# The second half of a retention gate, moved from the attention stage into a Strassen stage of its own

## The chip, the cores and the metric

The program runs on one core of one Trainium2 chip. The metric is the device time of one execution in microseconds (us). An execution has a TensorE queue (PE in the profile; its weight loads are PEld), VectorE (DVE), ScalarE (ACT), GpSimd (POOL), and SyncE (SP), which here only issues transfers. Every wait between engines is a semaphore written by hand in the source.

## The reference

A layer of a language model on 1024 tokens of width 1024, in fp32: a norm, one wide projection `proj = hn @ w_in`, a retention branch and a sliding-window attention branch, each with gates, and an MLP behind them.

```
hn = rms_norm(h, mix_norm_g)
proj = hn @ w_in
rq, rk, rv, rg, sq, sk, sv, gr, gs = split(proj)   # widths 512, 512, 1024, 1024, 1024, 256, 256, 1024, 1024
y_ret = rms_norm(retention(rq, rk, rv)) * silu(rg)
y_swa = sliding_window_attention(sq, sk, sv, sinks)   # 16 query heads, 4 key heads, window 128, 16 meta tokens
merged = sigmoid(gr) * (y_ret @ w_ret_branch) + sigmoid(gs) * (y_swa @ w_swa_branch)
h = h + merged @ w_out
h = h + square(relu(rms_norm(h) @ w_up)) @ w_down
```

The change concerns `rg`, of which `silu(rg)` is stored in a DRAM tensor `gates`.

## The kernel before

**Arithmetic.** An fp32 product is made of three matmuls (`three`, L1144 to 1151): high part by high part, high by low, low by high. So each weight tile exists twice, as WH (rounded by a ScalarE copy) and WL (the rest, a VectorE subtraction); both are rings of eight tiles of 128 x 512. A slab is 512 columns of `w_in`, k is one of eight blocks of 128 input channels, and a slab by all tokens is 64 steps of three matmuls of 512 columns: 192.

**Stages.** The first slab (RQ) runs to about 51 us. From there to 290.8 us comes the Strassen stage: three pairs of slabs (`NSG = 3`: RK with the keys and values of the attention, the two halves of RV, the two halves of SQ), each as the seven products of one Strassen step (`st_product`, L1216) of four bands f, four k and three matmuls, 48 matmuls a product. Quarters of the weights are loaded by SP into PX, PY, PZ and RAW; VectorE forms their sums in PX, PZ and PT (`add_y`, `st_sum`, `add_raw`) and WL (`st_lo`), ScalarE forms WH (`st_hi`). Results are copied out of the banks by ScalarE (`evict`), or summed by VectorE (`result`) in the tiles SA and SB, and stored by GpSimd (`store_st`) to `proj`. Next comes the retention stage, to about 430 us, which weaves the two GR slabs (SLAB_B) between its blocks n = 0 to 7; then `BR = 36` gate steps ahead; then the attention stage from about 457 to 720 us. The last stages, to 1608 us, are the two branches, `w_out`, and the MLP as Strassen products of larger size.

**The attention stage.** It has 68 steps T. A step of TensorE is: its share of the gate slabs GS, GS + 512, RG, RG + 512 (`SLAB_D = 3` to 6; `gate_steps`, L119, spreads 4 x 64 - 36 = 220 gate steps of three matmuls evenly, three or four in each T), the values of a group of two pairs (`values`, odd T), transposes of the next queries or keys, the transposes of the probabilities of pair T - 3 (`transpose_p(T - LAG)`, L1431 and L1434), and the scores of pair T (`scores(T)`, L1417). A pair is two of 16 heads in one of eight blocks of 128 tokens, 64 pairs. VectorE does the minimum over sinks and scores (L2716), the reciprocal of the sum (L2749), the low part of the transposed probabilities (L2724), the splits of the gate weights (L2252), and for `rg` the product of the gate (`tanh` + 1) x value. ScalarE does exponentials (L2012), tanh and casts.

GpSimd's loop, in this order in each T (L1017 to 1043): scale the two heads' probabilities by the reciprocal (L1023); store finished gate tiles (L960); in T = 9, 17, ..., 49 load a table of distances; in T = 20, 28, 36, 44 load KV (L969); in odd T from 7 two transfers that add values to RT from YA (L1042). SP copies the scaled probabilities PR to PW (`copy_p`, L783), which `transpose_p` waits for. These transfers are issued in program order, and an issuing engine does nothing else meanwhile.

## Time and profile before

| | us |
|---|---|
| time, median of 3 runs | 1610.26 (1610.2 to 1610.85) |
| the profiled execution | 1610.03 |
| its span, first to last instruction | 1608.2 |
| mean granted clock | 1.00 |
| TensorE busy | 1599.7 (99%) |
| VectorE busy | 1045.2 (65%) |
| ScalarE busy | 773.2 (48%) |
| GpSimd busy | 420.9 (26%) |

The span lies inside the time; what is around it is start and end of the program. Busy times are those of the profiled execution. A matmul is shown longer than the distance to the next, since matmuls overlap in the array; their distance is read from the starts in the timeline. A transfer's busy time on its engine is the time of issuing it; its landing is told apart.

### The profile page before, as it was taken

What the parts mean: (1) busy time and instruction counts of PE and PEld (TensorE: products, weight loads), DVE (VectorE), ACT (ScalarE), POOL (GpSimd) and SP (SyncE); (2) the same over time, 40 slices, a digit from 0 to 9 for tenths busy, and PEclk for the clock granted to TensorE, in tenths of its full rate; (3) what the DMA queues carried; (4) which work ended last, traced back from release to release, by engine and by line L of the source; (5) the groups of instructions that cost most, each with busy time, mean ns of one, the idle gap of its engine ahead of it and who ended that gap; (6) DMA issues with size and microseconds to landing.
All of it is one profiled execution on the core that took longest, in us unless ns stands there. A gap on an engine that the chain in (4) does not pass through costs nothing.

```text
span 1608.2 us, 22700 instructions
## 1 busy us (share of the span) xinstructions
PE 1599.7 (99%) x7966; PEld 1338.7 (83%) x7966; DVE 1045.2 (65%) x2015; ACT 773.2 (48%) x1587; POOL 420.9 (26%) x604
## 2 busy tenths in 40 slices
PE   9999999999999999999999999999999999999999
PEld 7888888888888888888888888888888888888887
DVE  7984656655657787766555338866666556756675
ACT  7633243545456777672122136655555444444442
POOL 0111011211348898864211000121121222100000
PEclk9999999999999999999999999999999999999999
DMA  8433332654435666568553223444444399733452
GB/s 300 180 101 120 100 117 72 234 181 167 156 117 152 171 177 165 159 153 269 174 186 96 66 82 115 136 166 150 144 150 158 118 322 351 243 94 97 154 180 92
DMA packets 129825, 255.95 MB, mean 159 GB/s; under 512 B 15040, under 2 KB 50288, under 8 KB 129712
## 3 DMA queue, kind: packets, MB, share of 16 engines
q1 hardware_dynamic: 84416, 130.64, 25.9%
q0 software_dynamic: 45008, 123.72, 23.2%
q8 instruction: 64, 1.05, 0.3%
q14 instruction: 49, 0.40, 0.1%
q10 hardware_dynamic: 288, 0.14, 0.0%
HBM read 159.67 MB, written 69.47 MB: 142 GB/s over the span
## 4 chain that ended last, share of the span: by engine, by line
PE 96%; DVE 2%; ACT 1%; DMA 1%; POOL 1%; issue 0%; DVEq 0%; ACTq 0%
PE bank L1146 29%; PE bank L1151 29%; PE bank L1150 29%; PE bank L1417 2%; PE bank L1449 1%; PE bank L1431 1%; PE bank L1189 0%; PE bank L1549 0%; PE bank L1335 0%; PE bank L1466 0%; PE bank L1499 0%; DVE WL L2252 0%; PE bank L1453 0%; POOL PR L1023 0%; PE bank L1434 0%
## 5 line engine op out<-in xcount | busy, mean ns | idle before, releaser
L1146 PE MATMUL bank<-WH,ADH 128*128 128x512 f32 x448 | 174.3, 389 | 0.0
L1150 PE MATMUL bank<-WH,ADL 128*128 128x512 f32 x448 | 174.3, 389 | 0.0
L1151 PE MATMUL bank<-WL,ADH 128*128 128x512 f32 x448 | 174.3, 389 | 0.0
L1146 PE MATMUL bank<-HN,WH 128*128 128x512 f32 x384 | 153.0, 398 | 0.1
L2178 ACT CAST ADH<-ARAW 128x512 fp32r<-128x512 f32 x112 | 69.6, 621 | 169.7 <-PE bank L1151 152.5
L1023 POOL TENSOR_SCALAR PR<-PR,RC 128x272 f32<-128x272 f32 (+1 forms) x128 | 138.4, 1216 | 47.5 <-DVE RC L2749 47.3
L1151 PE MATMUL bank<-HN,WH 128*128 128x512 f32 x384 | 150.2, 391 | 0.0
L1150 PE MATMUL bank<-HN,WL 128*128 128x512 f32 x384 | 150.1, 391 | 0.0
L3003 DVE TENSOR_TENSOR ADL<-ARAW,ADH 128x512 fp32r<-128x512 f32 x112 | 77.5, 692 | 97.2 <-ACT ADH L2178 97.2
L1146 PE MATMUL bank<-SOPH,WH 128*128 128x512 f32 x256 | 99.8, 390 | 0.0
L1151 PE MATMUL bank<-SOPL,WH 128*128 128x512 f32 x256 | 99.6, 389 | 0.0
L1150 PE MATMUL bank<-SOPH,WL 128*128 128x512 f32 x256 | 99.6, 389 | 0.0
L1146 PEld LDWEIGHTS bank<-WH,ADH 128*128 128x128 f32 x448 | 84.1, 188 | 17.6
L1151 PEld LDWEIGHTS bank<-WL,ADH 128*128 128x128 f32 x448 | 84.1, 188 | 17.5
L1150 PEld LDWEIGHTS bank<-WH,ADL 128*128 128x128 f32 x448 | 84.1, 188 | 17.3
L2012 ACT ACTIVATE PR<-PR,NM 128x273 f32<-128x273 f32 (+1 forms) x128 | 64.3, 504 | 55.2 <-DVE NM L2716 54.9
L1151 PEld LDWEIGHTS bank<-HN,WH 128*128 128x128 f32 x384 | 72.1, 188 | 16.0
L1146 PEld LDWEIGHTS bank<-HN,WH 128*128 128x128 f32 x384 | 72.3, 188 | 13.1 <-DVE TB L2744 0.5
L1150 PEld LDWEIGHTS bank<-HN,WL 128*128 128x128 f32 x384 | 72.3, 188 | 11.9
L2144 ACT CAST WH<-XS 128x512 fp32r<-128x512 f32 x64 | 39.1, 616 | 87.4 <-DVE XS L2970 45.1
L1104 POOL DMA_DIRECT2D uop<-UA x48 | 26.0, 541 | 192.8 <-ACT UA L2231 96.0
L1146 PE MATMUL bank<-A,WH 128*128 128x512 f32 x192 | 74.9, 390 | 0.0
(360 smaller groups left out, 4308.1 us busy)
## 6 DMA issues: line engine op xcount, KB each, us to landing
ARAW<-uop SPq DMA_DIRECT2D x112, 256.0 KB, 3.1
uop<-US POOLq DMA_DIRECT2D x64, 256.0 KB, 2.9
WRAW<-in_w_up SPq DMA_DIRECT2D x15, 1024.0 KB, 6.2
PW<-PR SPq DMA_DIRECT2D x56, 272.0 KB, 3.0
RAW<-in_w_in SPq DMA_DIRECT2D x58, 256.0 KB, 4.1
gates<-TB POOLq DMA_DIRECT2D x48, 256.0 KB, 2.7
uop<-UA POOLq DMA_DIRECT2D x48, 256.0 KB, 3.1
proj<-SA POOLq DMA_DIRECT2D x36, 256.0 KB, 2.6
```

Source lines behind the costliest of these rows:

```text
L1023: pr = pool.tensor_scalar(keys, keys, RC[:, b, hl:hl + 1], None, ALU.mult)
L1104: pool.dma_start(uop[t, f], src[:, :]).then_inc(ust_a, 16)
L1146: mm = pe.matmul(bank, ahi, bhi, start=first, stop=False, skip_group_check=onto)
L1150: pe.matmul(bank, alo, bhi, start=False, stop=False, skip_group_check=onto)
L1151: return pe.matmul(bank, ahi, blo, start=False, stop=last, skip_group_check=onto)
L1417: mm = pe.matmul(B[2 + hl][:, 0:NKEY if n else NKEY0], QT[:, 2 * p + hl, :], KTS[:, part, g, keys_of(n, hl)], start=part == 0, stop=part == 1)
L1431: pe.transpose(B[4][:, c * P:(c + 1) * P].bitcast(F32R), PW[:, b, key:key + P], IDR[:, :])
L1449: pe.matmul(B[7][:, :], v, tile[:, sl, :, :].rearrange("p h t -> p (h t)"), start=opens, stop=True, skip_group_check=not opens)
L2012: e = act.activation(part, part, ACT.Exp, scale=-1.0, bias=NM[:, T % 3, hl:hl + 1], accum_out=RS[:, T % 3, hl:hl + 1])
L2144: act.copy(WH[:, wslot(q), :].rearrange("p (k n) -> p k n", k=4), up_src(f, t)).then_inc(uw_hi, 1)
L2178: act.copy(ADH[:, n % 4, :], ARAW[:, n % 4, :]).then_inc(da_hi, 1)
L3003: dve.tensor_tensor(ADL[:, n % 4, :], ARAW[:, n % 4, :], ADH[:, n % 4, :].bitcast(F32), ALU.subtract)\
```

## The change

`SLAB_E` falls from 7 to 6: the attention stage holds three gate slabs instead of four, `NGT = 24` gate tiles instead of 32, and 3 x 64 - 36 = 156 gate steps instead of 220, two or three in each T instead of three or four. The columns RG + 512 to RG + 1023 are computed behind the three pairs of the Strassen stage and ahead of the retention stage, as a fourth pair `GX` of two halves of 256 columns. Its seven products (`gx_product`) have two bands f of 128 output columns, four k and three matmuls each, 24 matmuls a product. Here the weights are the stationary operand and 512 tokens move through, so that a result is a tile of 128 output columns by 512 tokens, as `gates` holds it. SP loads quarters of 256 columns (PYX, RAW, PXX, PZX); the sums, splits, evictions, tanh and products of this part run on the engines that did the same before, with tiles SA and SB, and GpSimd stores eight tiles to `gates[5]` (`store_gx`), between the loads of the first retention tiles (`load_rt`), one of which moves behind a store. The split of the first retention slab (SLAB_B) moves behind it. In block n = 0 the retention stage has two added waits on TensorE and two on ScalarE. Semaphore targets and the ring's numbering follow.

```
--- before.py
+++ after.py
-SLAB_B, SLAB_D, SLAB_E, SLAB_F, SLAB_H = 1, 3, 7, 11, 13
+SLAB_B, SLAB_D, SLAB_E, SLAB_F, SLAB_H = 1, 3, 6, 10, 12
...
+GX, GXF = NSG, 2
+NSX = NSG + 1
+W0 = NSX * NST
 BR = 36
+
+NGT = 8 * (SLAB_E - SLAB_D)
...
-    n = 4 * KT * 8 - BR
+    n = NGT * KT - BR
     return range(BR + n * T // STEPS, BR + n * (T + 1) // STEPS)
...
-ASIDE = (4, 5, 6)
+ASIDE = (4, 5)
...
+GX_EVICT = {0: 0, 2: 1, 3: 2}
+GX_SUM = {1: 0, 4: 1, 5: 2}
+GX_OUT = {1: 0, 4: 1, 5: 2, 6: 3}
+GX_HALF = {1: 0, 4: 1, 5: 0, 6: 1}
...
+        PXX, PTX = at("PXX", O_M, [4, 256]), at("PTX", O_M + 4096, [2, 256])
+        PYX, PZX = at("PYX", O_M + 8192, [4, 256]), at("PZX", O_M + 16384, [4, 256])
...
+            if g == GX:
+                return (PXX[:, k, :], RAW[:, k, 0:256], PTX[:, k % 2, :], PXX[:, k, :], PTX[:, k % 2, :],
+                        PZX[:, k, :], PTX[:, k % 2, :])[t]
...
+        def st_w(tile, g, t, k):
+
+            return tile[:, st_n(g, t, k) % WS, 0:256 if g == GX else SL]
+
+        def gx_act_of(t, k):
+
+            if t in QUAD:
+                return SHI[:, QUAD[t], k, :], SLO[:, QUAD[t], k, :]
+            k, lo = (k + 4, SL) if t == 6 else (k + 4 * t, 0)
+            return HN[:, 0, k, lo:lo + SL], HN[:, 1, k, lo:lo + SL]
+
+        def gx_bank(t, f):
+
+            return B[4 + f] if t % 2 == 0 else B[2 + f]
+
+        def gx_tile(t, f):
+
+            return SB[f] if t in (2, 5) else SA[2 + f] if t == 6 else SA[f]
...
+            done = 20 * (NSG - 1)
+            c0, c1 = COL_RG + SL, COL_RG + SL + 256
+            sp.wait_ge(ps_x, done + XT4 + 4)
+            sp.dma_start(PYX[:, :, :], quarter(c1, 0, 256)).then_inc(py_full, 16)
+            sp.wait_ge(ps_x, done + ZS + 4)
+            for k in range(4):
+                sp.dma_start(RAW[:, k, 0:256], w_in[SL + k * P:SL + (k + 1) * P, c0:c0 + 256]).then_inc(raw_full[k], 16)
+            sp.wait_ge(ps_x, done + XT6 + 4)
+            sp.dma_start(PXX[:, :, :], quarter(c0, 0, 256)).then_inc(px_full, 16)
+            sp.dma_start(PZX[:, :, :], quarter(c1, 1, 256)).then_inc(pz_full, 16)
+            sp.wait_ge(ps_x, 20 * GX + ZS + 4)
...
-            w_from = [w_cols(w_in, COL_GS), w_cols(w_in, COL_GS + SL), w_cols(w_in, COL_RG), w_cols(w_in, COL_RG + SL)] \
+            w_from = [w_cols(w_in, COL_GS), w_cols(w_in, COL_GS + SL), w_cols(w_in, COL_RG)] \
...
+            def store_gx(t):
+                for f in range(GXF):
+                    pool.wait_ge(gx_out, gx_at(GX_OUT, t, f))
+                    pool.dma_start(gates[5, GX_HALF[t], f + (GXF if t in (4, 5) else 0)], gx_tile(t, f)[:, :])\
+                        .then_inc(gx_st[t][0], 16)
+
+            store_gx(1)
...
             load_rt(0)
-            pool.wait_ge(c_full, CF0)
-            pool.wait_ge(pst_b, PSB0)
-            pool.wait_ge(c_sq, st_stat(NSG - 1, 5, 3) + 1)
-            pool.dma_start(MASK[:, :], c_mask).then_inc(c_full, 16)
-            store_st(NSG - 1, 6)
-            for n in range(1, 4):
+            store_gx(4)
+            load_rt(1)
+            store_gx(5)
+            for n in range(2, 4):
                 load_rt(n)
+            store_gx(6)
...
+            def gx_product(t):
+                for f in range(GXF):
+                    if t == 0:
+                        pe.wait_ge(ps_dve, 12 * (NSG - 1) + 8 + 2 + f + 1)
+                    elif t == 1:
+                        pe.wait_ge(ps_act, 16 * (NSG - 1) + 12 + 2 + f + 1)
+                    elif t in (2, 4):
+                        pe.wait_ge(gx_evicted, GE0 + gx_at(GX_EVICT, t - 2, f))
+                    elif t == 3:
+                        pe.wait_ge(gx_sum, GS0 + gx_at(GX_SUM, 1, f))
+                    elif t == 5:
+                        pe.wait_ge(gx_evicted, GE0 + gx_at(GX_EVICT, 3, f))
+                    else:
+                        pe.wait_ge(gx_sum, GS0 + gx_at(GX_SUM, 4, f))
+                    fs = slice(f * P, (f + 1) * P)
+                    for k in range(4):
+                        if f == 0:
+                            pe.wait_ge(w_ready, st_n(GX, t, k) + 1)
+                        w = st_n(GX, t, k) % WS
+                        mm = three(gx_bank(t, f)[:, :], WH[:, w, fs], WL[:, w, fs], *gx_act_of(t, k),
+                                   k == 0 and t not in (2, 4, 6), k == 3, f == 0 and k == 0, t in (2, 4, 6))
+                        if f == GXF - 1 and k < 3:
+                            mm.then_inc(w_free, 1)
+                    mm.then_inc(gx_full, 1)
+
+            for t in range(7):
+                gx_product(t)
...
+                    if n == 0:
+                        pe.wait_ge(gx_sum, PD0)
...
+            def gx_gate(t, f):
+
+                if t == 6:
+                    act.wait_ge(gx_full, GF0 + gx_at(range(7), t, f))
+                    source = gx_bank(t, f)
+                else:
+                    act.wait_ge(gx_sum, GS0 + gx_at(GX_SUM, t, f))
+                    source = gx_tile(t, f)
+                if t > 1:
+                    act.wait_ge(gx_out, gx_at(GX_OUT, t, f) - GXF)
+                act.activation(SA[2 + f][:, :], source[:, :], ACT.Tanh, scale=0.5).then_inc(gx_tanh, 1)
...
+            def gx_swish(t, f):
+
+                dve.wait_ge(gx_tanh, gx_at(GX_OUT, t, f))
+                if t == 6:
+                    source = gx_bank(t, f)
+                else:
+                    dve.wait_ge(gx_sum, GS0 + gx_at(GX_SUM, t, f))
+                    source = gx_tile(t, f)
+                dve.scalar_tensor_tensor(out=gx_tile(t, f)[:, :], in0=SA[2 + f][:, :], scalar=1.0, in1=source[:, :],
+                                         op0=ALU.add, op1=ALU.mult).then_inc(gx_out, 1)
...
+            def gx_sums(t):
+
+                st_sum(GX, t, 0)
+                st_sum(GX, t, 1)
+                st_lo(GX, t, 0)
+                st_sum(GX, t, 2)
+                st_lo(GX, t, 1)
+                st_sum(GX, t, 3)
+                st_lo(GX, t, 2)
+                st_lo(GX, t, 3)
+
+            for k in range(4):
+                st_lo(GX, 1, k)
+            for k in range(4):
+                add_y(GX, k)
+            gx_sums(2)
+            for f in range(GXF):
+                gx_result(1, f)
+            for k in range(4):
+                st_lo(GX, 3, k)
+            for f in range(GXF):
+                gx_swish(1, f)
+            gx_sums(4)
+            for f in range(GXF):
+                gx_keep(f)
+            for k in range(4):
+                st_lo(GX, 5, k)
+            for k in range(4):
+                add_raw(GX, k)
+            for f in range(GXF):
+                gx_result(4, f)
+            gx_sums(6)
+            for f in range(GXF):
+                gx_swish(4, f)
+            for f in range(GXF):
+                gx_result(5, f)
+            for k in range(4):
+                split_lo(SLAB_B, k)
+            for f in range(GXF):
+                gx_swish(5, f)
+            for f in range(GXF):
+                gx_swish(6, f)
```

VectorE at the end of the Strassen stage. SB and SA are result tiles, WL low parts, KD the first tile of the retention stage (the first line of both is the end of a product of the stage, the last the start of the retention stage). Before:

```order
L2372 TENSOR_TENSOR SB3_110<-bank5,SB3_110 128x512
L2392 TENSOR_REDUCE RQS_111<-JK_102 128x8
L2252 TENSOR_TENSOR WL_67<-RAW_68,WH_66 128x512 x4
L2392 TENSOR_REDUCE RQS_111<-JK_102 128x8 x2
L2513 TENSOR_TENSOR KDM_124<-MRK_93,COLS_82 16x512
L2392 TENSOR_REDUCE RQS_111<-JK_102 128x8 x3
L2252 TENSOR_TENSOR WL_67<-RAW_68,WH_66 128x512 x3
L2539 TENSOR_TENSOR KD_119<-RT_51,COLS_82 128x512
```

Now, the last part of the added stage and the same start of the retention stage (PTX, PZX: sums of 256 columns):

```order
L2677 TENSOR_TENSOR SA0_103<-SA0_103,bank4 128x512
L2677 TENSOR_TENSOR SA1_104<-SA1_104,bank5 128x512
L2509 TENSOR_TENSOR PTX_127<-PXX_126,PZX_129 128x256 x2
...
L2679 TENSOR_TENSOR SB0_107<-bank2,SB0_107 128x512
L2679 TENSOR_TENSOR SB1_108<-bank3,SB1_108 128x512
L2401 TENSOR_TENSOR WL_67<-RAW_68,WH_66 128x512 x4
L2694 SCALAR_TENSOR_TENSOR SB0_107<-SA2_105,SB0_107 128x512
L2694 SCALAR_TENSOR_TENSOR SB1_108<-SA3_106,SB1_108 128x512
L2694 SCALAR_TENSOR_TENSOR SA2_105<-SA2_105,bank4 128x512
L2694 SCALAR_TENSOR_TENSOR SA3_106<-SA3_106,bank5 128x512
L2401 TENSOR_TENSOR WL_67<-RAW_68,WH_66 128x512 x3
L2759 TENSOR_TENSOR KD_119<-RT_51,COLS_82 128x512
```

The split of the retention's first slab now stands between results and products of the gate, and the last results of `gates[5]` ahead of the second half of that split.

TensorE in the attention stage, one even step near the middle, from the scores (L1417) of the step ahead to the transposes of the probabilities PW (L1431); bank0 takes gate steps, KST are keys of the next block. Before:

```order
L1417 MATMUL bank3<-KTS_165,QT_164 128x272 x2
L1146 MATMUL bank0<-HN_49,WH_66 128x512
L1150 MATMUL bank0<-HN_49,WL_67 128x512
L1151 MATMUL bank0<-HN_49,WH_66 128x512
L1146 MATMUL bank0<-HN_49,WH_66 128x512
L1150 MATMUL bank0<-HN_49,WL_67 128x512
L1151 MATMUL bank0<-HN_49,WH_66 128x512
L1146 MATMUL bank0<-HN_49,WH_66 128x512
L1150 MATMUL bank0<-HN_49,WL_67 128x512
L1151 MATMUL bank0<-HN_49,WH_66 128x512
L1474 MATMUL bank5<-IDR_166,KST_143 128x128 x4
L1431 MATMUL bank4<-IDR_166,PW_140 128x128 x4
```

Now, the step that answers to it:

```order
L1518 MATMUL bank3<-KTS_169,QT_168 128x272 x2
L1215 MATMUL bank0<-HN_49,WH_66 128x512
L1219 MATMUL bank0<-HN_49,WL_67 128x512
L1220 MATMUL bank0<-HN_49,WH_66 128x512
L1215 MATMUL bank0<-HN_49,WH_66 128x512
L1219 MATMUL bank0<-HN_49,WL_67 128x512
L1220 MATMUL bank0<-HN_49,WH_66 128x512
L1575 MATMUL bank5<-IDR_170,KST_147 128x128 x4
L1532 MATMUL bank4<-IDR_170,PW_144 128x128 x4
```

Three matmuls are gone from between the scores of one pair and the transposes of an earlier one.

GpSimd from T = 19 on (PR scaled by RC; YA added to RT; KV loaded; gates stored). Before:

```order
L1042 DMA RT_51<-YA0_158 64x2x128 x2
L1023 TENSOR_SCALAR PR_151<-PR_151,RC_155 128x272 x2
L969 DMA KV_137<-proj 128x4x64 x2
L1023 TENSOR_SCALAR PR_151<-PR_151,RC_155 128x272 x2
L1042 DMA RT_51<-YA1_159 64x2x128 x2
L1023 TENSOR_SCALAR PR_151<-PR_151,RC_155 128x272 x2
L960 DMA gates<-TB_74 128x512
```

Now:

```order
L1109 DMA RT_51<-YA0_162 64x2x128 x2
L1090 TENSOR_SCALAR PR_155<-PR_155,RC_159 128x272 x2
L1027 DMA gates<-TB_74 128x512
L1036 DMA KV_141<-proj 128x4x64 x2
L1090 TENSOR_SCALAR PR_155<-PR_155,RC_159 128x272 x2
L1109 DMA RT_51<-YA1_163 64x2x128 x2
L1090 TENSOR_SCALAR PR_155<-PR_155,RC_159 128x272 x4
```

The scalings, the transfers from YA and the loads of KV are as many as before; the stores of gates are fewer and fall into other steps, here into one with a load of KV.

## Rows read from the trace of the kernel before

**Rows 1.** The page: engine, busy us, share of span, count.
```profile
PE 1599.7 (99%) x7966; PEld 1338.7 (83%) x7966; DVE 1045.2 (65%) x2015; ACT 773.2 (48%) x1587; POOL 420.9 (26%) x604
```

**Rows 2.** Waits of PE: what waited for what, us in total, times, longest.
```profile
PE bank L1431 <- DMA PW<-PR: 0.7, 1, 0.7
```

**Rows 3.** Timeline of PE: start, duration, instruction; Strassen stage, then attention.
```profile
262.17 0.39 PE L1146 MATMUL bank<-WH,SHI 128*128 128x512 f32 x1
...
267.61 0.39 PE L1146 MATMUL bank<-WH,SHI 128*128 128x512 f32 x1
...
563.88 0.40 PE L1146 MATMUL bank<-HN,WH 128*128 128x512 f32 x1
...
566.61 0.40 PE L1449 MATMUL bank<-PTH,KVR 128*128 128x512 f32 x1
```

**Rows 4.** Stretches: length; busy (count) of PE, PEld, DVE, ACT, POOL; clock; DMA.
```profile
220.00:240.00 20.00, 20.00 (x90) 16.55 (x89) 11.87 (x20) 8.53 (x16) 2.16 (x4) 1.00 0.14 53
520.00:560.00 40.00, 40.00 (x251) 34.93 (x249) 28.72 (x92) 28.74 (x76) 35.17 (x39) 1.00 0.61 159
560.00:600.00 40.00, 40.00 (x250) 34.94 (x249) 33.23 (x100) 29.96 (x80) 36.52 (x40) 1.00 0.65 175
640.00:680.00 40.00, 39.48 (x241) 33.71 (x240) 32.62 (x97) 28.24 (x76) 33.84 (x35) 1.00 0.60 158
```

**Rows 5.** Groups by line and form: busy us, mean ns of one, idle before.
```profile
L2652 DVE TENSOR_TENSOR KVR<-KV,KVR 128x256 fp32r<-128x256 f32 x6 | 2.5, 418 | 0.7 <-ACT KVR L1929 0.7
...
L2372 DVE TENSOR_TENSOR SB<-bank,SB 128x512 f32<-128x512 f32 x4 | 2.7, 685 | 0.8 <-PE bank L1151 0.8
...
L1781 ACT COPY SA<-bank 128x512 f32<-128x512 f32 x14 | 8.2, 585 | 17.2 <-PE bank L1151 16.6 <-DMA proj<-SA 0.6
...
L1869 ACT ACT_TABLE_LOAD x1 | 1.3, 1283 | 0.0
```

**Rows 6.** Timeline of all engines, the attention stage; in brackets idle time before.
```profile
560.71 2.78 POOL L1023 TENSOR_SCALAR PR<-PR,RC 128x272 f32<-128x272 f32 x2 [1.93 <-DVE RC L2749]
...
587.88 0.74 PE L1417 MATMUL bank<-KTS,QT 128*128 128x272 f32 x4
...
591.95 0.15 DVE L2749 RECIPROCAL RC<-RS 128x2 f32<-128x2 f32 x1
...
592.21 1.91 POOL L1023 TENSOR_SCALAR PR<-PR,RC 128x272 f32<-128x272 f32 x2 [1.16 <-DVE RC L2749]
...
594.08 1.98 POOL L1042 DMA_DIRECT2D RT<-YA  x2
...
595.89 2.12 POOL L1023 TENSOR_SCALAR PR<-PR,RC 128x272 f32<-128x272 f32 x2
...
598.03 0.51 SPq L783 DMA_DIRECT2D PW<-PR  x1
...
598.39 1.70 POOL L969 DMA_DIRECT2D KV<-proj  x2
...
603.31 0.51 PE L1431 MATMUL bank<-IDR,PW 128*128 128x128 f32 x4
...
603.75 0.73 PE L1417 MATMUL bank<-KTS,QT 128*128 128x272 f32 x4
```

**Rows 7.** The transfer's line in the attention stage: ns min/median/max, then its landings.
```profile
L783 SPq DMA_DIRECT2D PW<-PR x58: 490/500/508, 481.1 to 710.0; - x58
...
DMA to landing us min/median/max: 2.3/3.0/4.9
```

**Rows 8.** Timeline of SP and PE: two pairs with little time between transfer and transposes.
```profile
496.69 0.50 SPq L783 DMA_DIRECT2D PW<-PR  x1
...
499.21 0.53 PE L1431 MATMUL bank<-IDR,PW 128*128 128x128 f32 x4 [0.67 <-DMA PW<-PR]
...
710.03 0.49 SPq L783 DMA_DIRECT2D PW<-PR  x1
...
713.35 0.46 PE L1431 MATMUL bank<-IDR,PW 128*128 128x128 f32 x4
```

154 lines of the change are left out of this document (109 added, 45 removed).

## Prediction

> **What bounds the kernel now.** I read the page's busy line first [rows 1]: TensorE is busy 99% of the span. Its list of waits is short, and only one of them lies in the attention stage: 0.7 us for one transfer PW<-PR [rows 2]. So at first sight the time is the number of matmuls times their spacing. But "busy" counts a matmul of 512 columns as 389 or 390 ns, while such matmuls start 0.227 us apart (24 spacings from 262.17 to 267.61) [rows 3]. Twelve of them in the attention stage take 2.73 us, so one gate step (three matmuls) costs 0.68 to 0.69; I use 0.685. A gap of up to 0.16 us would not show. The second look is therefore at the table of stretches [rows 4]. In the Strassen stage the other engines are half idle. In the attention stage GpSimd is busy 34 to 36.5 us of 40 and VectorE 29 to 33. Every term below follows from this: the change fills the first stage and empties TensorE in the second.
>
> **What is removed.** 64 gate steps leave the attention stage: 64 x 0.685 = 43.8 us of TensorE, 0.94 step (0.645 us) in each of 68 steps. With them go eight weight splits and eight gate products of VectorE, eight casts and eight tanh of ScalarE, eight stores of GpSimd and eight weight loads of SP. None of these is waited for by TensorE there, so they are worth nothing by themselves.
>
> **What is added.** Seven products of two bands, four k and three matmuls: 168 x 0.2267 = 38.1 us [rows 3]. A plain slab is 192; the difference is the whole gain, 43.8 - 38.1 = 5.7 us. Does the new stage run at TensorE's pace? A product lasts 5.44 us instead of 10.88. VectorE has 44 operations of 256 columns (the nearest row is 418 ns [rows 5]) and 16 of 512 columns (0.69): 18.4 + 11.0 = 29.4 us in 38.1. ScalarE has 24 casts of 256 columns, six evictions and eight tanh of about 0.6, and one more table load of 1.3 (later a second, when the square root comes back): some 20 us. Laying them one after another behind the bands they wait for, each product's last weight tile is ready about 2 us or more before it is read: the ring of eight tiles frees a slot half a product early. The first retention tile is loaded after the fifth product, 10.9 us before its use, over twice the longest landing in [rows 7]. SP's loads are half as large as those that arrived in time for the pairs before. I cost all this at nothing, with the half idle engines as cover; if a wait of 0.3 us came at every product it would be 2 us.
>
> **Where the cover ends: the attention stage.** A pair of heads goes scores (TensorE), minimum (VectorE), exponential (ScalarE), reciprocal (VectorE), two scalings (GpSimd), transfer PW<-PR (SP), transposes (TensorE), and the transposes stand three steps after the scores. One loop, in the rows of steps 34 to 38 [rows 6]: scores at 587.88, reciprocal 591.95, scalings 592.21, GpSimd's two accumulating transfers RT<-YA from 594.08 (2.0 us), the next pair's scalings until the transfer is issued at 598.03. It lands 3.0 us later (median of 58; 2.3 to 4.9 [rows 7]), transposes take 0.44, and the scores of step 38 can start at 601.5. That is 13.6 us for four steps. They stood at 603.75: TensorE took 15.9 and hid the loop. Without 4 x 0.645 = 2.6 it takes 13.3, and the loop is longer. A load of KV in GpSimd's queue (1.7 us) or a gate store comes on top in some steps.
>
> The same by pairs: from issue to transposes the 56 pairs of full width have 2.53 to 6.46 us, median 5.2, so less 3.0 a margin of 2.2; three steps lose 3 x 0.645 = 1.94, and 23 of the 56 margins are smaller. The tightest are in [rows 8]: step 9 (issued 496.69, transposed 499.21 after the wait of 0.67) and step 63 (710.03, 713.35). I went through all 64 pairs in order: a pair's wait is what its three steps lose less its margin, counted from the delay already there at its scores. The delay grows by 0.7 at the start, 2.6 at steps 11 and 12, 1.0 at 20, 2.1 at 29 to 32, 0.6 at 36, 1.0 at 44, 2.2 at 51 and 52, 1.3 at 64, some tenths between: 12.0 us. With the shortest landing, 2.3 us, for every pair it is 5.2; with 3.3 it is 16. Two things move it. VectorE's backlog near steps 29 and 50 comes from weight splits that leave or move (less, perhaps 3 us). GpSimd works 3.4 to 3.65 us in each step against TensorE's new 3.35; it loses only 0.08 per step of stores, so its queue lengthens (more). They roughly cancel, and I keep 12: this lies near the row for the median, and both ends stay for the range.
>
> **Sum.** 1608.2 - 43.8 + 38.1 + 12.0 = 1614.5 us of span. The profiled execution took 1610.03 with a span of 1608.2, so 1.8 lies around it, and the median shown is 0.2 above that: 1616.5 us, 0.4% slower.
>
> **A rule against this.** By the rows, LDWEIGHTS fills 34.9 us of 40 in the middle of the attention stage, more than VectorE, and at its two ends about as much as GpSimd [rows 4]. The Trainium skill (Perfetto Trace Analysis, section Identifying the Most-Contended Engine) says to judge TensorE by that share and to speed up the engine with the highest occupancy. Read so, TensorE and GpSimd tie, and if TensorE counted, the gain would come whole. That is the first rival. The rule looks at sums; the loop above at latency.
>
> **Rivals.** First, *the cover holds*: the transfers land earlier, and VectorE's lighter queue shortens the chain, so fewer than 2.6 us are waited. For it: GpSimd idles 3.5 to 6 us of 40 now, step 63's margin was already only 0.3 without a wait, and the clusters of splits go. Against it: one pair already waited, and 23 margins are too small. Then 1608.2 - 5.7 + 2 + 2.0, about 1604.5 to 1607. Second, *half of it*: the wait is 2.6 to 8 us, as with the landing of 2.3 us for all. The time is 1607 to 1612.5, mostly no difference that can be told. Third, *the slow side beyond the forecast*: GpSimd's queue sets the pace. Its scalings (1.9 us for a pair, up to 2.8 where they run beside VectorE [rows 6]) slow down because VectorE is denser, and at 3.6 to 3.7 us per step instead of 3.35 over some 56 steps the wait is 14 to 20 us; it decides from about 16 us of wait, and gives 1620.5 to 1625. Fourth, *the new stage doesn't do what it says*: VectorE, with 29.4 of 38.1 us, is late for the products after its sums (third, fifth, seventh). Each would have to be late by over 2 us before TensorE waits at all; 3 us in all would make 1619.5. I count it within the third.
>
> **Chances.** Forecast (8 to 16 us waited, 1612.5 to 1620.5): 0.50. Cover holds: 0.22. Half of it: 0.17. Beyond: 0.11. A measurement of this kernel can tell about 0.2% (3.2 us) from no change. Faster by more than that is the first rival, 0.22. Within it lie the second and the lowest edge of the forecast, 0.22. Slower is the rest, 0.56. The range goes from the first rival's time, 1604.5, to the top of the forecast, 1620.5; it leaves out the third and fourth. The forecast's own range is 1612.5 to 1620.5.
>
> **What would show it.** In the profile after: 168 new matmuls 0.227 us apart over about 38 us with no wait of TensorE in front of them (the new stage is free), and the retention stage as long as before. In the attention stage, waits of TensorE's transposes and their weight loads on PW<-PR adding up to about 12 us, the steps at 3.5 us on average instead of 3.95, GpSimd busy over 95% between the waits. The forecast is wrong if the step falls to 3.35 and the list of waits stays under 3 us (first rival), or if TensorE waits for WL or a bank in the new stage (fourth), or if the landing stays 3.0 us but the chain from scores to issue shrinks by more than a microsecond.

## The result, and the profile after

The changed kernel takes **1630.83 us** (median of four, 1630.58 to 1632.93) against 1610.23 (1609.98 to 1610.85) before: ratio 1.013, 95% interval 1.0113 to 1.0148. It is 20.6 us slower. The forecast was 1616.5, the range ended at 1620.5.

The page of the changed kernel, its busy line and two of its groups, beside [rows 1]:

```profile
span 1628.8 us, 22773 instructions
...
PE 1602.8 (98%) x7942; PEld 1335.1 (82%) x7942; DVE 1063.5 (65%) x2063; ACT 783.7 (48%) x1615; POOL 418.2 (26%) x604
...
L1090 POOL TENSOR_SCALAR PR<-PR,RC 128x272 f32<-128x272 f32 (+1 forms) x128 | 144.6, 1335 | 33.1 <-DVE RC L2969 32.7
...
PW<-PR SPq DMA_DIRECT2D x56, 272.0 KB, 2.8
```

TensorE is "98% busy", which again tells next to nothing. GpSimd's 128 scalings take 144.6 us, 6.2 more than before for the same work. The list of TensorE's waits, which answers to [rows 2]:

```profile
PE bank L1532 <- DMA PW<-PR: 11.3, 14, 2.1
PE bank L1550 <- issue: 3.5, 9, 0.9
PE bank L1318 <- DVE EPSC L2411: 2.0, 1, 2.0
PE bank L1215 <- DVE SML L2791: 1.7, 1, 1.7
PE bank L1215 <- DVE WL L2401: 1.2, 1, 1.2
PE bank L1423 <- ACT QS L2025: 0.9, 1, 0.9
...
PE bank L1532 <- DVE PTL L2944: 0.6, 1, 0.6
PE bank L1428 <- DVE KD L2759: 0.2, 1, 0.2
```

L1532 are the transposes of PW, L1550 the values, L1423, L1428 and L1215 with SML the first block of the retention stage. The wait for WL lies far behind the attention stage, at 923 us. These rows make 19.4 us beside the 2.0 at the program's start; the list leaves out what hides in the 0.16 us by which matmuls overlap. So I read the stages from the starts of TensorE's instructions: the first retention matmul (L1399 after, L1302 before), the first scores, the last transposes of probabilities, and the end of the last matmul.

| stretch, us | before | changed | difference |
|---|---|---|---|
| to the first retention matmul | 290.8 | 328.7 | +37.9 |
| retention, gate steps ahead | 166.8 | 169.5 | +2.7 |
| attention stage | 256.0 | 236.4 | -19.6 |
| the rest | 891.3 | 890.9 | -0.4 |

One gate step (0.685) of the 64 left the second stretch, 62 the third, one the fourth. So the retention stretch waits 3.4 us more. The work of the attention stage alone is 256.0 - 62 x 0.685 = **213.5**; it takes 236.4 and waits **22.9 us** more than before, where the sum had 12. The last stretch is 0.2 us longer than its gate step less makes it. Together: 37.9 - 43.8 + 3.4 + 22.9 + 0.2 = 20.6.

The table of stretches, which answers to [rows 4] (length; busy and count of PE, PEld, DVE, ACT, POOL; clock; DMA share; GB/s):

```profile
291.00:329.00 38.00, 38.00 (x168) 31.23 (x167) 28.40 (x64) 19.91 (x45) 5.51 (x10) 1.00 0.36 119
540.00:580.00 40.00, 38.46 (x250) 32.90 (x249) 29.17 (x97) 28.33 (x79) 36.58 (x41) 1.00 0.64 168
580.00:620.00 40.00, 37.80 (x236) 32.01 (x235) 30.60 (x99) 28.40 (x78) 36.14 (x41) 1.00 0.62 162
620.00:660.00 40.00, 35.98 (x228) 30.39 (x227) 32.92 (x100) 31.32 (x84) 36.02 (x40) 1.00 0.57 148
```

The first row is the new stage: 168 matmuls in 38.0 us, VectorE busy 28.4, ScalarE 19.9, no wait. The other three are the attention stage: TensorE has gaps in each, where before only one stretch of [rows 4] had any (39.48 of 40), and no other engine is full either.

### The profile page after: what moved, and what is told of

It reads as the page before. It is cut to its first block, busy times and chain, and to the rows that moved or that the text cites. A ratio compares the mean times of both kernels' runs of the same rounds, so it can differ in the third digit from the quotient of the medians.

```text
span 1628.8 us, 22773 instructions
## 1 busy us (share of the span) xinstructions
PE 1602.8 (98%) x7942; PEld 1335.1 (82%) x7942; DVE 1063.5 (65%) x2063; ACT 783.7 (48%) x1615; POOL 418.2 (26%) x604
## 4 chain that ended last, share of the span: by engine, by line
PE 84%; DVE 5%; DMA 4%; POOL 4%; ACT 2%; issue 1%; ACTq 0%; DVEq 0%
PE bank L1215 27%; PE bank L1220 27%; PE bank L1219 27%; POOL PR L1090 2%; DMA PW<-PR 1%; ACT PR L2161 1%; DMA RT<-YA 1%; POOL RT L1109 1%; DMA gates<-SA 1%; DVE PTL L2944 1%; DVE PR L2936 1%; DVE QNF L2855 1%; ACT PTH L2138 0%; PE bank L1650 0%; PE bank L1258 0%
## 5 line engine op out<-in xcount | busy, mean ns | idle before, releaser
L1215 PE MATMUL bank<-WH,ADH 128*128 128x512 f32 x448 | 174.3, 389 | 0.0
L1090 POOL TENSOR_SCALAR PR<-PR,RC 128x272 f32<-128x272 f32 (+1 forms) x128 | 144.6, 1335 | 33.1 <-DVE RC L2969 32.7
L1215 PE MATMUL bank<-HN,WH 128*128 128x512 f32 x344 | 137.3, 399 | 0.0
L1220 PE MATMUL bank<-HN,WH 128*128 128x512 f32 x344 | 135.2, 393 | 0.0
L1219 PE MATMUL bank<-HN,WL 128*128 128x512 f32 x344 | 135.0, 392 | 0.0
L1215 PE MATMUL bank<-SOPH,WH 128*128 128x512 f32 x256 | 99.8, 390 | 0.0
L1215 PEld LDWEIGHTS bank<-WH,ADH 128*128 128x128 f32 x448 | 84.1, 188 | 17.5
L1220 PEld LDWEIGHTS bank<-HN,WH 128*128 128x128 f32 x344 | 64.8, 188 | 14.2
L1215 PE MATMUL bank<-A,WH 128*128 128x512 f32 x192 | 74.9, 390 | 0.0
L1219 PE MATMUL bank<-A,WL 128*128 128x512 f32 x192 | 74.7, 389 | 0.0
L1220 PE MATMUL bank<-A,WH 128*128 128x512 f32 x192 | 74.7, 389 | 0.0
## 6 DMA issues: line engine op xcount, KB each, us to landing
ARAW<-uop SPq DMA_DIRECT2D x112, 256.0 KB, 3.0
uop<-US POOLq DMA_DIRECT2D x64, 256.0 KB, 3.0
RAW<-in_w_in SPq DMA_DIRECT2D x52, 256.0 KB, 4.6
uop<-UA POOLq DMA_DIRECT2D x48, 256.0 KB, 3.2
gates<-TB POOLq DMA_DIRECT2D x40, 256.0 KB, 2.7
proj<-SA POOLq DMA_DIRECT2D x36, 256.0 KB, 2.3
```

Of the source, the lines that this page charges most:

```text
L1090: pr = pool.tensor_scalar(keys, keys, RC[:, b, hl:hl + 1], None, ALU.mult)
L1215: mm = pe.matmul(bank, ahi, bhi, start=first, stop=False, skip_group_check=onto)
L1219: pe.matmul(bank, alo, bhi, start=False, stop=False, skip_group_check=onto)
L1220: return pe.matmul(bank, ahi, blo, start=False, stop=last, skip_group_check=onto)
```

## Experiments

Each is a short edit of the changed kernel unless it says so. "Stage" is the attention stage, from the first scores to the last transposes, and "retention stretch" is what lies ahead of it from the first retention matmul on; both are read from the one profiled execution. Four runs that leave the attention stage alone (changed, e4, e8, e11) have it at 235.8 to 237.1, so a difference of 1 us there says little. Cover is the work that TensorE has of its own while an item is away on other engines. Times are medians of four runs (e15: of ten) against 1610.0 to 1610.2 for the kernel before on the same chip.

| run | time | ratio (95%) | retention stretch | stage |
|---|---|---|---|---|
| changed kernel | 1630.8 | 1.013 (1.0113 to 1.0148) | 169.5 | 236.4 |
| e1 before, thinned | 1588.6 | 0.9867 (0.9852 to 0.9882) | 166.5 | 237.7 |
| e2 direct | 1626.5 | 1.0096 (1.0079 to 1.0113) | 171.9 | 230.6 |
| e3 no accumulation | 1624.5 | 1.0097 (1.0075 to 1.0119) | 171.6 | 228.6 |
| e4 stores first | 1631.6 | 1.0133 (1.0118 to 1.0148) | 171.3 | 236.6 |
| e5 stores on SP | 1628.2 | 1.0112 (1.0096 to 1.0127) | 170.2 | 231.0 |
| e6 odd steps | 1634.8 | 1.0155 (1.0138 to 1.0172) | 168.9 | 240.3 |
| e7 first steps | 1636.5 | 1.0165 (1.015 to 1.018) | 171.4 | 238.9 |
| e8 QS first | 1634.0 | 1.0145 (1.013 to 1.016) | 172.4 | 237.1 |
| e9 both | 1621.6 | 1.0072 (1.0057 to 1.0087) | 169.6 | 224.2 |
| e10 short splits | 1630.1 | 1.0128 (1.0113 to 1.0143) | 171.9 | 235.5 |
| e11 loads last | 1627.2 | 1.0105 (1.009 to 1.012) | 166.1 | 235.8 |
| e12 BR = 32 | 1632.0 | 1.0135 (1.0118 to 1.0152) | 169.0 | 238.6 |
| e13 before, cover -25 | 1597.5 | 0.992 (0.9905 to 0.9935) | 166.7 | 245.1 |
| e14 before, cover -50 | 1593.8 | 0.9897 (0.9882 to 0.9911) | 166.1 | 241.2 |
| e15 both, no low part | 1612.9 | 1.0016 (1.0006 to 1.0025) | 171.4 | 215.7 |
| e16 e5 and e11 | 1622.8 | 1.0075 (1.006 to 1.009) | 166.1 | 231.2 |

### Which part of the change costs (e1)

```
-SLAB_B, SLAB_D, SLAB_E, SLAB_F, SLAB_H = 1, 3, 7, 11, 13
+SLAB_B, SLAB_D, SLAB_E, SLAB_F, SLAB_H = 1, 3, 6, 10, 12
...
-    n = 4 * KT * 8 - BR
+    n = NGT * KT - BR
```

> The kernel before with the 64 gate steps of the second half of RG left out (its attention stage as thin as in the changed kernel, with its order of loads), and no new stage. The half of the gate is not computed; the other half is read twice. Theory A (the waits in the attention stage come from thinning that stage alone): 43.8 us less TensorE work and about 23 us more waiting there, so 1610.3 - 43.8 + 23 = 1589.5, within 1587 to 1592, and the attention stage, from first scores to last transposes of probabilities, again near 236 us instead of 256. Theory B (the new stage, or what it does to the loads and stores behind it, brings a good part of the waiting): under 1584, with an attention stage under 230 us.

Measured 1588.6, stage 237.7: theory A. Whoever thins the stage gets 21.4 us for 43.8, new stage or not. (What e1 keeps of the change is its order of loads, so this run doesn't separate the thinning from that order; e13 and e14 do.) The other half of the account, the new stage itself, is the 37.9 us of the table.

### The stage: how the time answers to the cover (e13, e14)

e13 (e14 without `i % 2 == 0`), in the kernel before:

```
-                pe.matmul(bank, alo, bhi, start=False, stop=False, skip_group_check=onto)
+                if not short:
+                    pe.matmul(bank, alo, bhi, start=False, stop=False, skip_group_check=onto)
...
+                          short=i >= BR and i % 2 == 0)
```

> The kernel before with one of the three matmuls (low weight by high activation) left out in every second gate step of the attention stage, 110 matmuls of 0.228 us, 25 us of TensorE; every load, split, store and semaphore stays. Theory C (a pair has a margin, and the first half of the cover comes out nearly free): 20 us or more are saved, 1585 to 1590. Theory D (the chains are tied so closely that each us taken out is paid back by half from the first on): 11 to 15 us saved, 1595 to 1599.

> The kernel before with that matmul left out in all 220 gate steps of the attention stage, 50 us of TensorE, as its only change. The changed kernel took 43.8 us out of the stage and got 20 back. Theory C: the second half of the cover is worth next to nothing, so 22 to 27 us saved in all, 1583 to 1588, within 4 us of the run before. Theory D: 25 saved, and twice what the run before saved. If the wait came not from the cover but from the moved loads and splits, over 35 us are saved, under 1575.

Of 25 us taken out, 12.7 were saved; of 50, 16.4. So the first half pays 50%, the second 15% (3.7 of 25). Neither theory has both: the first run is D's (11 to 15 us), the second is C's in lying within 4 us of the first, and for the second both had expected 22 us or more. No load or split had moved, so the missing cover alone makes waits. The waits of e14:

```profile
PE bank L1433 <- DMA PW<-PR: 10.8, 15, 1.8
PE bank L1451 <- issue: 5.2, 10, 1.1
...
PE bank L1146 <- DVE WL L2254: 2.0, 3, 0.9
...
PE bank L1433 <- DVE PTL L2726: 1.2, 2, 0.9
PE bank L1476 <- ACT QT L1959: 1.0, 1, 1.0
```

The first two are the changed kernel's: PW, and the values (L1451). The tail is not: in its attention stage the changed kernel waits for no WL, no QT and for PTL only once, 0.6 us. e14's granted clock also fell twice, the changed kernel's once. e1, with 6 us less taken out than e14, saved 5 us more, 21.4 of 43.8. There splits, stores and tanh went with the matmuls, and e14's waits for WL and QT are missing; that this is the reason is likely and not shown. So a return that falls is shown only for matmuls taken out by themselves; thinned with all that belongs to it, the stage gave half back at 43.8 us as well.

### The stage: which chains (e2, e3, e9, e15)

e2, and e3:

```
-                        keys = PR[:, b, pr_keys((T - 1) // 8, hl)]
-                        pr = pool.tensor_scalar(keys, keys, RC[:, b, hl:hl + 1], None,
+                        to = PW[:, (T - 1) % 2, where.start - 1:where.stop - 1]
+                        pr = pool.tensor_scalar(to, keys, RC[:, b, hl:hl + 1], None,
...
-                        pool.dma_start(y_place(G, par), y_part(G, 1, par), accum_op=ALU.add)\
```

> The changed kernel; GpSimd's scaling writes its result straight into PW, rounded, and the transfer PW<-PR is left out, so that the low part of the probabilities is lost. It takes some 3.2 us out of the loop from scores to transposes and not a nanosecond out of GpSimd's queue. Theory A1 (latency of the loop): the waits of the transposes for PW (15 us) fall under 2, and the time falls by 13 to 20 us, to 1611 to 1618. Theory A2 (GpSimd's queue sets the pace): the transposes wait for the scaling instead, and the time stays above 1624.

> The changed kernel without GpSimd's 60 accumulating transfers RT<-YA (the second half of the values is not added); ScalarE's copies of the values then wait for SP's first transfer instead of theirs. It takes 2 us out of GpSimd's queue in every second step, some 60 us of its 202, and changes no other latency. Theory A2 (queue): GpSimd never stands in the way, the waits fall by more than 15 us, to 1611 to 1616. Theory A1 (latency): only the steps in which the two transfers stand directly ahead of the scaling get shorter; the time falls by 4 to 10 us, to 1621 to 1627.

Both theories had it as one bound, and each met a number and missed the other. In e2 the time stayed above 1624, as A2 had it, but not by A2's way: the transposes did not wait for the scaling instead. In e3 the time, 1624.5 (1623.0 to 1631.2), lies in A1's range of 1621 to 1627, while A1 was far off in e2 (4.3 us of 13 to 20). The direct scaling took 5.8 us off the stage; the waits for PW, 15.3 us by the starts of the matmuls, fell to 3.8, but those of the values rose from 6.0 to 9.5. The list puts the waits of the values down to "issue", but in 12 of the changed kernel's 13 places with over 0.1 us of it the first matmul of the values starts 0.10 us after VectorE's PTL ends. This is e2's list for them, and for the other place in which TensorE now waited:

```profile
PE bank L1550 <- issue: 7.5, 11, 1.5
...
PE bank L1532 <- DVE PTL L2944: 2.7, 3, 1.7
```

Without the accumulating transfers the stage lost 7.8 us, though GpSimd was busy only 24 to 28 us of 40. 15.1 us of waiting stayed, so GpSimd's queue alone isn't the bound. Part of those 7.8 need not be GpSimd's queue: ScalarE's copy of the values waits for such a transfer to land, in order, ahead of the exponential (5.2 us in four places, none in e3), and the chain that ended last runs over one of them. How much of the 7.8 it is, no run tells. The piece of that chain, and the timeline of the changed kernel around its longest gap in the stage:

```profile
526.96 6.29 DMA RT<-YA
```

```profile
526.31 2.13 POOL L1109 DMA_DIRECT2D RT<-YA  x2
...
527.64 2.76 POOL L1090 TENSOR_SCALAR PR<-PR,RC 128x272 f32<-128x272 f32 x2
...
530.43 4.72 SPq L840 DMA_DIRECT2D PW<-PR  x2
...
533.33 0.59 ACT L2146 COPY YA<-bank 128x512 f32<-128x512 f32 x1 [1.62 <-DMA RT<-YA]
...
534.24 0.54 PE L1532 MATMUL bank<-IDR,PW 128*128 128x128 f32 x4 [2.08 <-DMA PW<-PR]
```

GpSimd issues the two accumulations, scales for 2.76 us beside a busy VectorE (1.91 in [rows 6]), SP issues the transfer at 530.43, it lands 3.8 us later, and TensorE has sat 2.08 us.

> The changed kernel with both of the edits made singly before: the scaling written straight into PW without the transfer (low part of the probabilities lost), and GpSimd's accumulating transfers left out (second half of the values not added). Singly they took 5.9 and 7.8 us off the stage of 236.4 us (work alone 213.5). Theory (several chains share the wait; with both relieved the one from transposes over ScalarE's rounding and VectorE's low part to the values is left, 9.5 us of wait in the run with the direct scaling): the stage takes 222 to 227 us. Rival (the loop over GpSimd is all there is): 213.5 to 217.

224.2 us: inside the range of the theory. The two gains nearly add, 12.2 of 13.6. Two links of one loop would add in the same way as two chains, so this sum doesn't tell them apart. What it does show is that 10.7 us stay with both gone. They lie on a path that I had left out of the forecast: transposes, ScalarE's rounding PTH, VectorE's low part PTL, and the values of the *next* step, whose bank of transposes is also needed again. It is not that chain alone: in six of the changed kernel's 13 places (3.7 of 5.8 us) VectorE had no idle time ahead of the PTL in question, but came straight from a weight split or a cast of transposed keys; in the other seven it stood idle for ScalarE's PTH.

```
-                dve.tensor_tensor(pair_part(PTL, n, pair), pair_bank(n), pair_part(PTH, n, pair).bitcast(F32), ALU.subtract)\
+                w = 8 if pair >= 12 else P
+                dve.tensor_tensor(pair_part(PTL, n, pair)[:, :, :, 0:w], pair_bank(n)[:, :, :, 0:w],
+                                  pair_part(PTH, n, pair)[:, :, :, 0:w].bitcast(F32), ALU.subtract)\
```

> The changed kernel with the direct scaling and without the accumulating transfers (stage 224.2 us), and with VectorE's low part of the transposed probabilities on 8 of 128 columns from pair 12 on (the rest keeps old values): 0.55 us less between the transposes of one step and the values and transposes of the next. Theory (that chain is what is left): the stage takes 213.5 to 218 us, the waits of the values under 2 us, time 1611 to 1616. Rival (the chain lies in ScalarE's queue or in the scores, and a shorter subtraction only moves the wait): 221 or more, time above 1618.

215.7, and two stretches of it:

```profile
540.00:580.00 40.00, 40.00 (x262) 35.07 (x261) 27.26 (x110) 31.04 (x86) 27.16 (x32) 1.00 0.28 83
620.00:660.00 40.00, 39.60 (x258) 34.35 (x257) 29.70 (x110) 33.60 (x92) 28.11 (x31) 1.00 0.27 77
```

TensorE is all but full again. 236.4 to 215.7 of 213.5: with the transfer, the accumulations and the low part all gone, 20.7 of the 22.9 us are accounted for. The last edit shortens the chain by 0.55 us a step, and it also takes about 23 us out of VectorE's queue; the two are not separated by a run. e10 below takes some 10 us out of that queue at other places and gains next to nothing. None of the three can be left out of a kernel that must keep its precision and its sum.

### The stage: queues and order (e5, e6, e7, e10, e12)

e5 moves the issues as they are from GpSimd's loop to SP's, behind `copy_p(T - 1)`, on other semaphores:

```
+                    for c in range(2):
+                        sp.dma_start(kv_half(KV, n + NKV, c), proj[4, n + NKV, :, c * 256:(c + 1) * 256].rearrange(
+                            "p (g d) -> p g d", g=4)).then_inc(kv2[n % 2], 16)
+                for i in gate_steps(T - 1) if 1 <= T < STEPS else ():
+                    if i % 8 == 7:
+                        sp.wait_ge(a_free, ACT_D + i // 8 + 1)
+                        sp.dma_start(gates[2 + i // 64, i // 8 % 8 // 4, i // 8 % 4], TB[:, i // 8 % 2, :])\
+                            .then_inc(gst2[i // 8 % 2], 16)
```

> The changed kernel with the gate stores, the KV loads and the distance tables of the attention stage issued by SP, behind its transfer PW<-PR, instead of by GpSimd. It takes about 25 us out of GpSimd's 202 in the stage and puts about 15 on SP. The direct scaling and the run without accumulating transfers took 5.9 and 7.8 us off the stage of 236.4, whose work alone is 213.5. Theory (several short chains share the wait, GpSimd's queue is one of them): a third to a half of what the accumulating transfers gave, 2 to 4 us, so 1627 to 1629. Rival (GpSimd's queue as a whole is what the stage goes by): the gain is in proportion to the time taken out, 25 of 60, but on the whole 23 us of waiting: over 6 us, under 1625.

1628.2 as the theory had it; but the stage alone lost 5.4, nearer the rival's 6 than the theory's 2 to 4, and in the profiled execution the new stage, the retention stretch and the end were each 0.7 longer, though the edit leaves them alone.

```
+    w = [30 if t % 2 else 18 for t in range(STEPS)]
+    at = [sum(w[:t]) for t in range(STEPS + 1)]
+    return range(BR + n * at[T] // at[-1], BR + n * at[T + 1] // at[-1])
```

> The changed kernel with its 156 gate steps spread 30 to 18 over odd and even T instead of evenly (3 or 2 in odd T, 1 or 2 in even T). In odd T the values wait for VectorE's low part of the probabilities transposed one step earlier (6 us in 14 steps); they would get 0.3 to 0.7 us more cover. Theory (this chain from one step's transposes to the next step's values is one of the bounds): that wait falls under 2 us and the time by 2 to 5, to 1626 to 1629. Rival (only the loop of three steps over GpSimd and the transfer counts, and a wait removed ahead of the values comes back at the transposes right behind them): within 1 us of 1630.8, with the waits for PW longer by as much as those of the values are shorter.

The waits of the values did fall (6.0 to 2.7), but those for PW rose from 15.3 to 18.3, and four us were lost: nearer the rival, and worse than it has it. About 1.6 us of this is a second fall of the granted clock, at 658 us, behind a wait of 1.75. e7 is the same edit with `w = [30 if t < 9 else 22 ...]`:

> The changed kernel with its 156 gate steps spread 30 to 22 over the first nine T and the others instead of evenly. The change stretched the slabs over more steps, so that the splits of the second gate slab fall into T = 9 to 12, where VectorE and ScalarE also norm and split the queries and keys of the next block; steps 10 to 12 took 4.1, 5.0 and 5.9 us. Here the splits come some two steps earlier. Theory (the collision costs most of these 5 us, and with it the fall of the granted clock behind the gap of 2.3 us): steps 8 to 13 together 3 to 5 us shorter, 1626 to 1628. Rival (the same waiting only moves, as every other step has less cover by then): within 1.5 us of 1630.8.

The time, 1636.5, is 5.7 us longer and outside both; 1.9 of it lie in the retention stretch, which the edit leaves alone. Steps 10 to 12 fell from 15.0 to 11.5 us, as the theory had it; but steps 0 to 7, where some five gate steps came on top, rose from 20.9 to 24.5, and steps 14 to 62 took 182.0 instead of 180.6 with fewer gate steps in them. Cover taken from where it was thin cost more here than it gave where nothing waited.

e10 puts 32 in the place of 512 columns in the splits:

```
+                    split_hi(slab, k, cols=32)
...
+                    split_lo(slab, k, cols=32)
```

> The changed kernel with the 19 weight roundings of ScalarE and the 17 to 19 subtractions of VectorE for gate weights in the attention stage done on 32 of the 512 columns (the other columns of WH and WL keep what they held), 0.6 us each less, some 10 to 11 us on each engine, most of it in steps 9 to 12 and 37 to 40. Theory (VectorE's and ScalarE's queues are in the loop as much as GpSimd's): 3 to 6 us off the stage, steps 10 to 12 together under 12 us instead of 15. Rival (GpSimd alone counts): under 1 us.

Stage -0.9, which is hardly outside the scatter, median time -0.7, and steps 10 to 12 take 15.1 as before: the rival. (The profiled execution was the slowest of the four, by 3.3 us over the median, so that the 0.9 is rough.) The collision with the splits, on which e7's expectation rested, was not the cause there; what e7 gained in these steps is then likely to come from the added cover ahead of them.

> The changed kernel with 32 gate steps ahead of the attention stage instead of 36, so that four more (2.7 us of TensorE) lie in the stage, one more in every seventeenth step. Theory (the stage is bound by its chains, and TensorE's work in it is filler): the stretch ahead gets 2.7 us shorter and the stage less than 1.5 us longer, so 1 to 2.5 us faster than 1630.8. Rival (the four steps ahead cover the first block's chain, or each step is paid in full inside): no change, or a wait at the first scores.

(`BR = 32`.) The stage got 2.2 us longer for 2.7 us of work, the rival's second case, as far as the scatter lets one say so. Why these four steps covered next to nothing stays open.

### The retention stretch (e4, e8, e11)

In the changed kernel TensorE waits there for ScalarE's QS (0.9) and VectorE's SML (1.7). Behind the second stands a store; the line of the stores of the new stage, and ScalarE's wait:

```profile
L999 POOL DMA_DIRECT2D gates<-SA x6: 540/542/557, 305.2 to 331.4; - x6
...
  ACT SMH L2048: 3.1, 1
...
DMA to landing us min/median/max: 2.3/4.7/12.7
```

```
             store_gx(5)
-            for n in range(2, 4):
-                load_rt(n)
             store_gx(6)
+            for n in range(2, 4):
+                load_rt(n)
```

> The changed kernel with the stores of the last two gate tiles issued ahead of the 1 MB loads of the third and fourth retention tile instead of behind them. In the changed kernel the last store landed 12.4 us after its issue, and ScalarE's rounding of SMK, which takes over its memory, waited 3.1 us for it, TensorE then 1.7. Theory: the store lands within about 6 us and this wait goes: 1.7 us less, 1628.5 to 1629.5. Rival: the transfers as a whole are the jam (about 400 GB/s for 15 us), the store lands no sooner for being issued first, and the time stays within 0.5 us of 1630.8.

The longest landing fell to 6.8 us, so the rival's reading of the transfers is out, but there was no gain: the wait for SML went, and QS waited 3.1 us instead of 0.9 (stretch 171.3). These two waits can't be put down to the edit. e2, e3, e7, e10, e12 and e15 leave this stretch alone, and in all of them QS waited 3.3 to 3.9 us and SML not at all, with a longest landing of 13.6 to 14.0. One of them, e2:

```profile
PE bank L1423 <- ACT QS L2025: 3.6, 1, 3.6
```

So the stretch has two ways of waiting without any edit, 168.9 to 170.2 us long in one and 171.4 to 171.9 in the other (e12 with its four steps added back), and e4 shows the earlier landing and no more. e8 moves `split_hi` and `split_lo` of SLAB_B, k = 4 to 6, behind QS and KD:

> The changed kernel with the order of stores as in the run before (last two gate tiles ahead of the third and fourth retention tile), and with ScalarE's copy of QS and VectorE's KD of block 0 ahead of the weight splits for k = 4 to 6 instead of behind them. With the stores alone moved, the wait for SML went and one of 3.1 us for QS came: QS stood behind splits whose weights were still on their way. Theory (an order that was harmless as long as the weights were there): from the first retention matmul to the first scores 166.2 to 167 us instead of 169.5 (171.3 with the stores alone moved), time 1627 to 1628.5. Rival (the transfers are late for TensorE too): it waits for WL at k = 4 instead, and nothing is gained.

The rival: TensorE waited for WL instead, 3.0 us in four places of this stretch (the expectation of the next run has 4.4, the sum over the whole program). The weights were late. e11:

```
+            for t in (4, 5, 6):
+                store_gx(t)
+            pool.wait_ge(w_hi, wn(SLAB_B, KT - 1))
+            for n in range(1, 4):
+                load_rt(n)
```

> The changed kernel with the stores of the added stage's tiles ahead of the 1 MB loads of retention tiles 1 to 3, and these loads issued only when the seventh of the eight GR weight tiles has been rounded. In the run with QS moved ahead of the splits TensorE waited 4.4 us for WL instead: the weights' transfers themselves were late. Theory (they share the transfer engines with the loads of the retention tiles, which in the kernel before came behind them): the waits for QS, SML and WL all go, 166.2 to 166.8 us from the first retention matmul to the first scores, time near 1627.5. Rival (the weights are late because their four places in RAW come free late, behind the added stage): QS still waits over 1 us, 168.5 or more.

166.1 us and not one wait in the stretch, below all that it takes by itself, and again in e16. So both waits were one cause: three loads of 1 MB, issued while the last GR weights and the last gate tiles were under way.

### The two repairs together (e16)

> The changed kernel with both repairs that leave nothing out: SP issues the attention stage's gate stores, KV loads and distance tables, and the loads of the retention tiles come behind the last GR weights. If they add: retention 166.1 us, stage about 231, time 1622 to 1624. It would still be slower than the kernel before by 12 us or more: the work saved by the change is 5.7 us, and the stage still waits some 17.

1622.8: they add, and it isn't enough. None of the versions tried that compute everything beats the kernel before, and this change could win 5.7 us of TensorE at most; e16's stage still waits 17.7.

## Why the prediction was wrong

- **What bounds the kernel, removed, added:** held. 37.9 us measured for the new stage against 38.1, without a wait in it; the busy share hid everything, and the gains are those of the sum (43.8 out, 38.1 in).
- **"I cost all this at nothing":** failed at its end, by 3.4 us. The working followed the added stage's own tiles, and they were in time. (For the first retention tile this was luck in part: its 10.9 us were held against the longest landing in [rows 7], of a transfer of 272 KB, while the 1 MB loads of these tiles took 6.8 to 14.9 us to land in the kernel before. It landed in 7.3.) It did not follow what stands behind it in the queues: the GR weights, whose first load was issued 25.9 us ahead of the retention stage before (265.0) and is issued 12.2 us ahead now (316.6), and the last gate tiles behind three loads of 1 MB (e11). The 3.4 is the profiled execution's; in the other way of waiting it is over 5 us.
- **The term of 12 us for the attention stage:** right in kind, half of the size (22.9). Its parts, from the starts of the matmuls, changed less before: transposes waiting for PW 14.5, values 5.4, the slower restarts and small gaps 2.4, the rest 0.6. The loop that I had worked out came to 14.5 against 12. The step that failed is the one in which the loop was taken to be the only chain: the values wait for PTL of the step before, a chain of one step that lost one step's cover, and with the loop relieved it takes over most of the wait that is left (e2, e9, e15). The working says that only one wait of TensorE's list lies in the attention stage. There were two, and the second is this one, at 646.8 us:

```profile
PE bank L1449 <- issue: 0.4, 1, 0.4
```

- **The margins were held fixed:** each pair's time to the issue was read from the trace of before. Over pairs 8 to 60 it grew on average from 6.70 to 7.11 us, of which 0.2 up to the minimum (VectorE works denser), 0.1 in the scalings (2.29 to 2.41) and 0.1 between reciprocal and scalings. The landing of the same pairs gave 0.1 of it back, 2.95 to 2.86.
- **"They roughly cancel":** wrong. The splits of VectorE and ScalarE together are worth 0.9 us or less, not 3 (e10); taking GpSimd's accumulations out gave 7.8 us of the stage and taking its stores and loads out 5.4 (e3, e5).
- **Rivals:** none reached the measured time. The first fell (the mean step is 3.58 us, not 3.35), and with it the second. The third had the right direction, but named GpSimd's queue as the one cause, and ended at 20 us of wait and 1625; the runs show at least two paths of nearly equal length, with waits for PW (14.5) and for PTL (5.4, and 9.5 once the first is relieved). The fourth, the new stage late for its own products, did not happen. The rule of the Trainium skill (Perfetto Trace Analysis, Identifying the Most-Contended Engine), by which the gain would have come whole, did not hold here: LDWEIGHTS filled 30.4 to 32.9 us of 40, GpSimd 36, and with GpSimd at 24 to 28 (e3) 15.1 us of waiting stayed.

## What to carry to other kernels

Where engines hand one item round in a loop, ask of every wait of TensorE how many steps of cover it has, and list them all: the one with a single step of cover can be the next bound even if it waits once, for 0.4 us, now. A stage whose engines are all 70 to 90% busy has no free margin to sell: of 25 us taken out of this one only half came off the time, of 43.8 with their loads and splits half, of 50 without them a third. Where one stretch takes 168.9 or 171.9 us in kernels that don't differ there, read a gain in another stretch from that stretch, not from the sum. And a stage put between two others must be followed to what it pushes back in each DMA queue, not only to its own tiles.

## What the runs showed of the hardware

**The granted clock fell behind gaps.** After the gap of 2.08 us the chip granted 0.66 in the next stretch, and matmuls started 0.43 us apart, the level of 1.2 GHz, instead of 0.23 (2.4 GHz):

```profile
530.00:535.00 5.00, 2.92 (x21) 2.50 (x20) 4.97 (x12) 3.38 (x10) 3.56 (x4) 1.00 0.52 155
535.00:540.00 5.00, 5.00 (x19) 3.95 (x18) 3.97 (x12) 4.36 (x13) 3.84 (x4) 0.66 0.52 108
```

```profile
535.51 0.40 PE L1219 MATMUL bank<-HN,WL 128*128 128x512 f32 x1
535.75 0.49 PE L1220 MATMUL bank<-HN,WH 128*128 128x512 f32 x1
536.04 0.63 PE L1215 MATMUL bank<-HN,WH 128*128 128x512 f32 x1
536.47 0.63 PE L1219 MATMUL bank<-HN,WL 128*128 128x512 f32 x1
```

It was back at 539.4. Eight matmuls at 0.2 us more are 1.6 us of the 22.9, and they count in TensorE's list as busy. So a long wait can cost more than its length. e14 had two such places, at 495 and 526, behind gaps of 1.77 and 1.75 us, and in seven runs (e2, e3, e4, e7, e10, e12, e15) it fell between 337 and 340 us, in or behind QS's wait of 3.1 us or more. The length of the last gap doesn't settle it: e4's gap of 2.26 us at 536 was followed by no fall, e11's of 1.5 at 530 was, and so were e8's four gaps of at most 1.0 at 335 to 341.

**A store behind large loads.** A tile of 256 KB stored by GpSimd lands 2.7 us after its issue (median, 40 stores of gates), and 12.7 us behind three loads of 1 MB, while the core's transfers ran at some 400 GB/s. Issued ahead of the last two of them, it landed in 6.8 us at most (e4), and with all three held back in 4.8 (e11).

**Scalings beside VectorE.** A pair of scalings of 128 x 272 takes 1.91 us at 592.21 with no weight split beside it, and 2.78 at 560.71 with two [rows 6]. Over the stage before, 38 pairs beside which VectorE has no `tensor_tensor` with both inputs in SBUF have a median of 2.04 us, the six with over 0.9 us of them 2.78. The Trainium skill (SBUF — State Buffer, section Who interferes with whom) says that the two engines share a port pair as an exclusive lock, and that a VectorE instruction with two SBUF inputs contends with a GpSimd instruction that reads SBUF. The trace before agrees as far as it goes. It isn't the whole: in the stage of the changed kernel the median of a single scaling rose from 1097 to 1427 ns, and 29 pairs with no such VectorE operation beside them have a median of 2.32, which this doesn't explain.
